# The second half of three output projections begins behind the last attention scores, for the first token tile

## The reference, cut to what matters

```
def fox_mixer(h, w_qg, q_norm_g, w_o, k, v, dcum):
    ...
    o = fox_attention(q, k, v, dcum).transpose(0, 2, 1, 3).reshape(B, S, D_MODEL)
    return (o * gate) @ w_o
def even_mixer(...):
    ...
    o = rmsnorm(o, subln) * (1.0 - lambda_init)      # end of diff_attention
    ...
    return jnp.concatenate([o_a, o_b], axis=-1) @ w_out
def odd_mixer(h, w_in, w_out, rel_bias):
    ...
    return chunk_band_attention(q, k, v, rel_bias) @ w_out
```

```
    x = x + rmsnorm(m.astype(x.dtype), g[3])
    h = rmsnorm(x, g[4])
    x = x + 0.5 * rmsnorm(swiglu_2(h, ffn_wg[l, 1], ffn_wu[l, 1], ffn_wd[l, 1]), g[5])
```

## Time and profile before

| | |
|---|---|
| time of the kernel before, median of 3 runs | 1793.18 us (1790.64 to 1793.9) |
| time of the profiled execution | 1792.04 us |
| its span | 1790.3 us |
| PE busy | 1718.8 us, 96% of the span |
| DVE busy | 1158.4 us, 65% |
| ACT busy | 893.7 us, 50% |

### The profile page before, as it was taken

The page is one execution under the profiler, slowest core; times in us unless marked ns, Lnnn a source line. Parts: engine busy times, 40 slices in busy tenths (PEclk is TensorE's granted clock), DMA queues, the critical chain, the costliest instruction groups (busy, mean ns, idle before and its releaser), DMA issues.

```text
span 1790.3 us, 22023 instructions
## 1 busy us (share of the span) xinstructions
PE 1718.8 (96%) x8926; PEld 1432.2 (80%) x8926; DVE 1158.4 (65%) x1604; ACT 893.7 (50%) x1268; POOL 7.4 (0%) x20
## 2 busy tenths in 40 slices
PE   5899999999999999999999989999999999999998
PEld 4797787878867888888888857888888889778887
DVE  7788888789656754565547966554665456675553
ACT  3465643374667444454444565444554445574442
POOL 0000000000000000000000000000000000000000
PEclk8999999999999999999999999999999999999999
DMA  8967487866713655555555314555554456345451
GB/s 350 401 254 280 167 350 294 341 273 234 275 53 123 243 217 184 208 188 182 174 194 191 121 68 154 187 176 186 194 208 177 176 206 229 118 143 182 172 198 47
DMA packets 54117, 363.43 MB, mean 203 GB/s; under 512 B 5744, under 2 KB 8944, under 8 KB 13056
## 3 DMA queue, kind: packets, MB, share of 16 engines
q1 hardware_dynamic: 52256, 351.47, 53.2%
q0 software_dynamic: 1760, 10.56, 1.5%
HBM read 360.95 MB, written 1.05 MB: 202 GB/s over the span
## 4 chain that ended last, share of the span: by engine, by line
PE 82%; DVE 9%; ACT 4%; DMA 3%; issue 1%; SPq 0%; POOL 0%; ACTq 0%; DVEq 0%
PE pp L601 79%; DVE low L1772 3%; DMA raw<-in_w 2%; PE pp L851 2%; DVE raw L1785 2%; PE pp L783 1%; DMA cst<-in_csts 1%; ACT wh L1268 1%; DVE tb L1772 1%; DVE hf L1916 1%; PE pp L927 1%; DVE x L1775 0%; DVE hl L1772 0%; DVE hidl L1772 0%; DVE tb L1775 0%
## 5 line engine op out<-in xcount | busy, mean ns | idle before, releaser
L1772 DVE TENSOR_TENSOR low<-raw,wh 128x2048 fp32r<-128x2048 f32 (+3 forms) x340 | 638.2, 1891 | 355.5 <-ACT wh L1268 355.1
L1268 ACT ACTIVATE wh<-raw 128x2048 fp32r<-128x2048 f32 (+3 forms) x346 | 535.8, 1567 | 436.2 <-PE pp L601 300.4
L601 PE MATMUL pp<-wh,hh 128*128 128x512 f32 x1312 | 521.6, 398 | 10.9 <-ACT hh L1298 6.1
L601 PE MATMUL pp<-low,hh 128*128 128x512 f32 x1312 | 514.5, 392 | 7.7 <-DVE low L1772 7.6
L601 PE MATMUL pp<-wh,hl 128*128 128x512 f32 x1312 | 507.5, 392 | 3.8 <-DVE hl L1772 3.7
L601 PEld LDWEIGHTS pp<-wh,hh 128*128 128x128 f32 x1312 | 247.8, 189 | 68.3 <-issue 14.4
L601 PEld LDWEIGHTS pp<-low,hh 128*128 128x128 f32 x1312 | 248.0, 189 | 59.5 <-DVE low L1772 10.3
L601 PEld LDWEIGHTS pp<-wh,hl 128*128 128x128 f32 x1312 | 247.6, 189 | 58.0 <-DVE hl L1772 5.8
L601 PE MATMUL pp<-low,hidh 128*128 128x512 f32 x592 | 230.8, 390 | 2.6 <-DVE low L1772 2.6
L601 PE MATMUL pp<-wh,hidh 128*128 128x512 f32 x592 | 232.0, 392 | 0.0
L601 PE MATMUL pp<-wh,hidl 128*128 128x512 f32 x592 | 230.6, 390 | 0.0
(11 more groups left out here) (201 smaller groups left out, 1162.9 us busy)
## 6 DMA issues: line engine op xcount, KB each, us to landing
raw<-in_w SPq DMA_DIRECT2D x314, 1024.0 KB, 4.8
raw<-in_w SPq DMA_DIRECT2D x24, 768.0 KB, 4.3
gain<-in_w POOLq DMA_DIRECT2D x6, 512.0 KB, 4.9
bT<-in_rel POOLq DMA_DIRECT2D x1, 2048.0 KB, 12.0
cst<-in_csts POOLq DMA_DIRECT2D x1, 1029.0 KB, 19.8
xT<-in_xT SPq DMA_DIRECT2D x1, 1024.0 KB, 7.8
binr<-in_bin POOLq DMA_DIRECT2D x1, 1024.0 KB, 10.9
wsT<-in_ws POOLq DMA_DIRECT2D x1, 1024.0 KB, 15.2
```

Source lines behind the costliest of these rows:

```text
L601: return e.matmul(out, lhsT, rhs, start=start, stop=stop, skip_group_check=True)
L1268: q.then_inc(e.activation(wh[j % NW][:, c], raw[i % NRAW][:, c], ACT.Copy), s_wh, (j, part))
L1772: return e.tensor_tensor(out, a, b, op)
```

## The change

Group 1's first four products of token tile 0 (its first piece, k 0 to 3, 12 matmuls) move from behind the attention into the filler's steps behind the last scores (i from 16 to 19), one a step. They write into the bank of the scores, for which PE first waits until DVE has read the last scores. `tail` then skips these four. In the even attention three empty filler steps ahead of the norm of `oa` go, and its rate is 2 from i = 15 on, so that all of group 0's first piece and the four products fit ahead of its end. On DVE, the whole piece of low weights that the early products need in the even stage (`ahead.out_early`) is made there.

```
-                self.steps, self.done = steps, set()
+                self.steps, self.done, self.scored = steps, set(), False
...
+                fill.scored = i >= len(steps)
...
         def even_rate(i):
-            return 3 if i < 6 else 1
+            return 3 if i < 6 else 1 if i < 15 else 2
...
-            def tile_by_tile(name, gi, js, src, at=()):
+            def tile_by_tile(name, gi, js, src, at=(), done=0):
...
-                            row_products(name, gi, j, k, m, src, pairs)
+                            if n >= done:
+                                row_products(name, gi, j, k, m, src, pairs)
                             n += 1
...
+            def out_early(kind):
...
+                name, hv = OUT_OF[kind]
+                cross((s_r,))
+                pairs.turn = 1
+                row_begin(name, 1, (s_y, (name, 1, 1)))
+                j = of_group[(name, 1)][0]
+                for k in range(items[pieces[j]][4]):
+                    row_products(name, 1, j, k, 0, h(hv), pairs)
+                    yield
...
                 for _ in range(4):
                     next(steps)
                     yield
+                while not fill.scored:
+                    yield
+                yield from out_early("even")
                 for _ in range(40):
                     yield
...
                 yield "bv"
-                for _ in range(4):
-                    yield
+                yield
                 yield
...
             def end_attention(name):
-                cross((s_r, t_r, o_r))
-                pairs.turn = 1
+                cross((t_r, o_r))
...
-            row_begin("even_out", 1, (s_y, ("even_out", 1, 1)))
-            tail("even_out", h(8))
+            tail("even_out", h(8), 4)
...
+            def out_early(self, name):
...
+                j = of_group[(name, 1)][0]
+                self.upto(j)
+                for _ in range(items[pieces[j]][4]):
+                    yield
```

More of the change, by code:

```diff
@@ L567, in each @@
             return all_of
+        OUT_OF = {"fox": ("o", 4), "even": ("even_out", 8), "odd": ("odd_out", 12)}
         NIBBLES = {"f": 2, "b": 1, "o": 1}
@@ L794, in turning, with tail @@
                 return work
-            def tail(name, src):
+            def tail(name, src, done=0):
                 js = of_group[(name, 1)][-2:]
@@ L800, in tail @@
                 first, then = (2 * n, 2 * n + 1) if NORMS[name]["early"] else (n + 5, n + 6)
-                tile_by_tile(name, 1, js, src, {first: [turning(name, 0, 0)], then: [turning(name, 0, 1)]})
+                tile_by_tile(name, 1, js, src, {first: [turning(name, 0, 0)], then: [turning(name, 0, 1)]}, done)
             def head(name, to, gi, end):
@@ L964, in fox_fill @@
                     yield
+                while not fill.scored:
+                    yield
+                yield from out_early("fox")
                 for _ in range(40):
@@ L1011, in odd_fill @@
                     yield
+                while not fill.scored:
+                    yield
+                yield from out_early("odd")
                 for _ in range(40):
@@ L1102, in tensor_program @@
             q.then_inc(mm(b[:, 0:2], ones[0:64, :], prod, True, True), s_aux, "lam")
-            row_begin("o", 1, (s_y, ("o", 1, 1)))
-            tail("o", h(4))
+            tail("o", h(4), 4)
             ffn(1, "o")
@@ L1176, in tensor_program @@
             pairs.ends[0] = fillp.ends.pop(0, pairs.ends[0])
-            row_begin("odd_out", 1, (s_y, ("odd_out", 1, 1)))
-            tail("odd_out", h(12))
+            tail("odd_out", h(12), 4)
             ffn(5, "odd_out")
@@ L1552, in out_steps @@
                     yield
+                while not fill.scored:
+                    yield
+                yield from ahead.out_early(name)
                 for _ in range(40):
```

## The result

The changed kernel took 1796.74 us (median of 15 runs, 1793.99 to 1800.27), the kernel before 1793.2 us (median of 15, 1789.32 to 1800.01). The ratio is 1.0024, with a 95% interval of 1.0016 to 1.0032: about 4.3 us slower (2.9 to 5.7). Its profiled execution took 1794.48 us, with a span of 1792.7 us, 2.4 us more than before.

The account below looks back on a forecast made before the run. PE was taken as busy almost throughout, with ACT's and DVE's way level with its products behind group 0. Terms 0.25 + 0.9 + 0.5 + 2.8 = +4.45 on 1793.18 gave 1797.6 us; own range 1795.3 to 1800, overall 1789.5 to 1801.5.

Parts of the forecast that it names:

- paid in full: Rival: ACT's and DVE's way behind group 0 can be shorter, all three stages give 2.75 us back; -8.1, 1785.1 us; chance 0.12.
- the clock up everywhere: Rival: fewer holes keep PE's clock up through the even stage too; -0.35, 1792.8 us; chance 0.12.
- waits without a fall: Rival: PE's new waits at the transposes come, but the clock stays up behind them; +1.65, 1794.8 us; chance 0.24.
- even worse: Rival: even norm's matmuls and work until group 0's end at half clock, all three waits followed by falls; +8, 1801 us; 0.12.
- The removal gives nothing, since ACT's and DVE's way is the bound: Behind group 0, the way to the transposes stays 8.9 us; PE waits about 2.75 us in even and odd, 2.3 in fox.
- Fox, +0.25: Fox attention's end: early products make group 0 end 0.7 us later, less 0.45 us of slack; +0.25 us.
- Odd, +0.9: Odd attention's end: early products make group 0 end 0.95 us later, less 0.05 us of slack; +0.9 us.
- Even until group 0's end, +0.5: Even attention's end: -1.5 us from moved work, +2.0 us from half the clock behind a wait for hh; +0.5 us.
- The clock behind the new waits, +2.8: Behind PE's waits at the transposes: half the clock costs 1.4 us each in even and odd, nothing in fox; +2.8 us.

Follow-up runs that it names:

- f2_reordered: Changed kernel; in even and odd the next layer's first weight piece made ahead of group 0's squares, the second behind tile 0's new x: 0.9997 of before.
- f1_next_before: Kernel before, with the first of the next layer's two weight pieces made ahead of group 0's squares in even and odd; no early products: 0.9997 of before.
- f3_even_norm: Kernel before with only the even filler's edits (norm of oa three steps earlier, rate 2 from iteration 15), no early products: 1.0005 of before.
- e5_keep_busy: Changed kernel with 9 (fox) or 11 (even, odd) unread matmuls of 128 x 512 on PE ahead of the first transposes: 1.0017 of before.

## Why the prediction was right

The forecast was 1797.6 us, or +4.45; the ratio gives +4.3. Its main step, that PE would only wait where the products had been, is shown. That the total came out so near is in part luck, since two of its terms were off by more than a microsecond in opposite directions. All four rivals lie outside the interval of +2.9 to +5.7 us: paid in full (-8.1), the clock up everywhere (-0.35), waits without a fall (+1.65, though that is what the even stage did), and even worse (+8). Term by term:

- **The removal gives nothing, since ACT's and DVE's way is the bound.** Right, and shown: the way was 8.86 in both stages as forecast (8.9), the waits 2.78, 2.78 and 2.05 us (forecast 2.75, 2.75, 2.3). `f2_reordered` showed the converse: once their way is shorter, the removal pays 2.7 us of it (8.65 in `f1_next_before`, 5.93 here). What a matmul costs shows in the rows above: one at 1592.79, the next at 1593.02, 0.23 us. (The prediction wrote 5.74 / 24 = 0.23; the quotient is 0.24, because the 5.74 us hold the last matmul's whole busy time. The 0.23 it went on with is right.) By the Trainium skill ("TensorE: Matmul & The Clock Gate", section "Wait — 56ns, not 53.3ns?") a warm matmul of 512 columns costs 215.7 ns, and twelve of them would be an estimated 2.6 us; the trace stands with 0.23.
- **Fox, +0.25: +0.5.** Group 0 came 1.0 us later behind the last scores (19.80 to 20.80), not 0.7, and 0.5 of it was slack, not 0.45. PE's last values started at 541.89, 7.33 us behind the scores against 6.37. The hand-laid holes were off by 0.3 us, less than half a product.
- **Odd, +0.9: +1.1.** 13.69 to 14.77 us, against 0.95 forecast.
- **Even until group 0's end, +0.5: +0.6 in this pair of profiles, about +1.6 between the means.** The steps were there: the last scores 2.5 us later (forecast 2.1), the wait for hh 3.84 (3.5), a clock of 0.51 behind it. But I set the sum against one execution of before, and that time varies by 3 us between profiles: the 33.62 of before lies 0.5 us above its list's mean, the 34.22 of the changed kernel 0.45 below its own. Against the means the term was too small by about a microsecond. In `f3_even_norm` the same stretch without the early products took 32.75 us, so of their 2.75 us some 1.5 to 2 are paid there.
- **The clock behind the new waits, +2.8: +1.5.** In odd it fell (1.5 us, forecast 1.4), in even it did not. This half of the term failed: I had given both waits one fate since they have one length. In fox the clock did fall, to 0.77 over the first 3 us, and cost nothing: tile 1's transposes came 8.45 us later, against 8.47 before, and 8.49 in `e5_keep_busy`, where the clock there was 1.00.

The last two errors nearly cancel: about 1.1 us too little in the even attention, 1.3 too much behind it. By stages the runs give fox and odd +2.9 (terms 0.25 + 0.9 + 1.4 = 2.55) and even +1.4 (0.5 + 1.4 = 1.9), each within its interval. The Trainium skill ("TensorE: Matmul & The Clock Gate", section "HAM oscillation — how this bites in real kernels") has the rule to order the work so that PE doesn't idle on a wait and stays warm. It is borne out as far as `e5_keep_busy` goes, which filled the wait with unread matmuls: the clock stayed at 1.00, and the spacing was 6.42 in place of 7.93. The change itself only moved PE's idle time into longer waits.

## What to carry to other kernels

Before work is moved from behind a point to ahead of it, lay the two ways that meet at the next hand-over side by side. Here PE's 13 products and the 8.9 us of ACT and DVE were level, so taking from either alone could only make a wait, and the work that moved ahead delayed the start of both. To gain on such a stretch, shorten both at once, and look next for the engine that then has no slack (DVE here, whose weight pieces took back 0.7 us a stage). Then add up what the moved work costs in its new place: no version here, the one with both ways shortened included, was shown to be faster than the kernel before. A term that hangs on where the clock falls is worth several profiles of the kernel before, not one.

## What I had not expected of the hardware

- A wait of PE of 2.78 to 2.79 us was followed by 3 us at 0.50 of the clock behind the odd attention (in two kernels) and by 1.00 behind the even one (in two kernels). The length of the wait alone doesn't tell which.
- The same instructions of the even attention's end took 31.31 us in one kernel and 33.62 in another that doesn't differ there, at a mean clock of 0.89 and of 0.80; with three kernels more, which have only a weight piece more on ACT and DVE there, the range is 31.31 to 34.30 us. In a kernel of 1793 us that is as large as most of what was measured here.
